# State products of the heads as 64-row tiles per head, on queries without zeros, even heads in one bank and odd heads in the other

## The chip, the cores and the metric

The kernel runs on one core of one Trainium2 chip. The metric is device time in microseconds of one execution; the time before is a median of three runs.

## The reference

One layer of a hybrid decoder over x (4096 tokens of 1024 values), cut here to what the change touches. The projection `h @ w_in` of the normalised input gives gated linear attention (GLA, 4 heads, 64 key and 128 value dimensions), a multi-scale pooling branch and a cross-attention into 256 memory tokens. The three are gated, concatenated, projected by `w_out`, added to x and normalised.

```python
# per head; chunks of 64 tokens; b = cumsum of the log decays in a chunk
q_d = q * exp(b)
k_d = k * exp(-b)
scores = tril(q_d @ k_d.T)                  # 64 x 64 in a chunk
o_intra = scores @ v
S_next = exp(b_last)[..., None] * S + k_end.T @ v   # S: 64 x 128
o_inter = q_d @ S                           # with the state before the chunk
o = o_intra + o_inter                       # then head RMSNorm, times silu(gate)
```

## The kernel before

The tokens go in 16 blocks of 256 (`TB`), each of 4 chunks of 64 (`NC`) and 2 halves of 128 tokens (`NT`). Blocks 0 to 3 are written out one by one and multiply whole weight matrices (`whole`, L683). Blocks 4 to 14 are one body in a loop on every engine, which multiplies by seven partial products a matrix (`phase` and `product`, L704); block 15 is written out with the tail behind it. The order on each engine is that of the code; engines wait for one another by semaphores.

The four heads are held as two pairs (`NPAIR`): of pair p, head 2p lies on partitions 0 to 63 and head 2p+1 on 64 to 127. Keys (`kd`), queries (`qb`) and the states `S[:, c, p, :]` (one for each chunk, 128 value columns) lie so. `qb` has a place for each head of a pair: `qb[:, p, h, :]` holds the decayed query of head h on its own 64 partitions and zeros on the other 64, which GpSimd writes once at the start (L2089). A product over all 128 partitions with `qb[:, p, h]` thus gives the one head alone.

In a block, TensorE (function `step`) works in this order behind the input products: values (`split`, L665), four transposes of `ke` (L866), the scores within chunks (L876, tiles of 64x64), scores against the memory (`mem_scores`, L892), a quarter of the output projection of the block before (`out_proj`, also L665), again L892, the chunk states (`states`, L903, tiles of 64x64), two more quarters, and then the stage that the change is about, `head_out`. For a pair p it multiplies the values by the masked scores `sT` (L912, o_intra, 4 products of f32) and the states by `qb` (L918, o_inter, 4 products of f32, 2 x 64 moving columns each), all added up in one bank: pair 0 in bank 5, pair 1 in bank 4. Behind it come the products of the memory attention (L971), the last quarter (L665) and the sums for the head norm (`head_ms`, L926).

ScalarE squares each of the two banks into `osq[p]` when the semaphore `pe_o` says so (L1425), and VectorE multiplies them by norm and gate into `mixed` (`head`, L1898 and L1900). VectorE makes `qb` (L1732), `ke` (L1735) and `kd` (L1737), and goes on with the states by `state` (L1889, semaphore `s_ok`). GpSimd waits for `pe_o` before it carries the last state over to the next block (L2138, L2139).

An f32 product of TensorE shows in the trace as two records of its line, each with its own weight load; so 4 products stand as x8.

Of the kernel before, what the change touches and what calls it, by code (L numbers as in the profile page):

```python
# [8 lines left out]
ALU = mybir.AluOpType  # L9
ACT = mybir.ActivationFunctionType  # L10
AX = mybir.AxisListType
F32 = mybir.dt.float32
# [4 lines left out]
P = 128  # L17
D = 1024
KT = D // P
TB = 256  # L20
NT = TB // P
CHUNK = 64
NC = TB // CHUNK
HEADS = 4
# [3 lines left out]
NPAIR = HEADS // 2  # L28
# [24 lines left out]
O_X, O_XS, O_MIX, O_T, O_U, O_QB = 0, 8192, 24576, 32768, 41216, 43392  # L53
# [55 lines left out]
def hybrid_block(nc, xt, x, memt, w_qk, w_v, w_qm, w_g, w_p, w_ut, w_gk_up, vecs, pool_w, counts, w_mem, w_out,  # L109
# [3 lines left out]
    with ctx:  # L113
# [3 lines left out]
        def sem(name):  # L117
            return ctx.enter_context(nc.semaphore(name))
# [33 lines left out]
        def view(off, shape, dt):  # L152

            size = int(np.prod(shape)) * (2 if dt in (F16, BF16) else 4)
            ap = arena[:, off // 4:(off + size) // 4]
            if dt != F32:
                ap = ap.bitcast(dt)
            if len(shape) == 2:
                ap = ap.rearrange("p (a b) -> p a b", b=shape[1])
            if len(shape) == 3:  # L160
                ap = ap.rearrange("p (a b c) -> p a b c", b=shape[1], c=shape[2])
            if len(shape) == 4:
                ap = ap.rearrange("p (a b c d) -> p a b c d", b=shape[1], c=shape[2], d=shape[3])
            return ap
# [8 lines left out]
        mixed = view(O_MIX, [KT, TB], F32)  # L173
# [4 lines left out]
        te = view(O_T + 6144, [2, TB], F32)  # L178
# [5 lines left out]
        pr = [view(O_T + 2048 * b, [2, NMEM], F32) for b in range(2)]  # L184
        phl = [view(O_T + 4096 + 2048 * b, [2, 2, NMEM], F16) for b in range(2)]
        ub = view(O_U, [2, HALO + TB], F32)
        qb = view(O_QB, [NPAIR, 2, TB], F32)
        kd = view(O_KD, [NPAIR, TB], F32)
        ke = view(O_KE, [NPAIR, TB], F32)
        osq = [view(o, [2, TB], F32) for o in (O_KD, O_KE)]  # L190
        v = view(O_V, [NT, 512], F32)
        gate = view(O_GATE, [KT, TB], F32)
# [4 lines left out]
        sT = view(O_ST, [NT, 2 * NPAIR, P], F32)  # L197
        S = view(O_S, [NC + 1, NPAIR, P], F32)
# [87 lines left out]
        bank = [ctx.enter_context(nc.psum_tensor(f"bank{i}", [P, 512], F32)) for i in range(8)]  # L286
# [10 lines left out]
        def col(n):  # L297
# [26 lines left out]
        built, ident_ok, zeroed, kept, mem_sq, mem_sum, mem_ms, mem_rs, mem_n = (  # L324
            sem(n) for n in ("built", "ident_ok", "zeroed", "kept", "mem_sq", "mem_sum", "mem_ms", "mem_rs",
                             "mem_n"))
# [13 lines left out]
        pe_o, pe_msq, pe_pv = (sem(n) for n in ("pe_o", "pe_msq", "pe_pv"))  # L340
# [6 lines left out]
        z_ok, gk_ok, b_ok, bl_ok, q_ok, dec_ok, kd_ok, ke_ok, pooled, y_add, y_ok = (  # L347
            sem(n) for n in ("z_ok", "gk_ok", "b_ok", "bl_ok", "q_ok", "dec_ok", "kd_ok", "ke_ok", "pooled",
                             "y_add", "y_ok"))
        sT_ok, max_ok, nmax_ok, rs_ok, s_ok, xn_ok, og_ok, mix_g, mix_m, mix_p, mmax_ok, m_lo = (  # L350
            sem(n) for n in ("sT_ok", "max_ok", "nmax_ok", "rs_ok", "s_ok", "xn_ok", "og_ok",
                             "mix_g", "mix_m", "mix_p", "mmax_ok", "m_lo"))
# [20 lines left out]
        def is_whole(i):  # L373
            return isinstance(i, int) and i < WHOLE
# [13 lines left out]
        def query(i):  # L388
            return qwhole if is_whole(i) else qtmp
# [212 lines left out]
        def _(pe):  # L602
# [146 lines left out]
            def step(i, first, second, last):  # L749
# [8 lines left out]
                for r in range(2):  # L758
                    for half in range(2):
                        for g in range(4):  # L760
                            k = 2 * g + half
                            b = 2 * (k // 4)
                            rhs = xs[:, 0, r, b:b + 2, (k % 4) * P:(k % 4 + 1) * P]
                            mm = nc.tensor.matmul(bank[3][32 * g:32 * g + 32, 0:TB], wlr[:, k, :], rhs,  # L764
                                                  start=r == 0 and half == 0, stop=r == 1 and half == 1)
# [13 lines left out]
                for j in range(2):  # L779
                    mm = nc.tensor.matmul(bank[5][:, j * TB:(j + 1) * TB], up4[:, j * P:(j + 1) * P],  # L780
                                          lrs[:, :], start=True, stop=True)
# [81 lines left out]
                for t in range(NT):  # L863
                    for p in range(NPAIR):
                        n = t * NPAIR + p
                        mm = nc.tensor.transpose(bank[4][:, n * P:(n + 1) * P], ke[:, p, t * P:(t + 1) * P],  # L866
                                                 ident[:, :])
                mm.then_inc(pe_ket, 1)
                for t in range(NT):
                    for p in range(NPAIR):  # L870
                        n = t * NPAIR + p
                        for odd in range(2):
                            for h in range(2):
                                r = slice(64 * h, 64 * h + 64)
                                c = slice((2 * t + odd) * CHUNK, (2 * t + odd + 1) * CHUNK)
                                mm = nc.tensor.matmul(bank[6 + h][64 * odd:64 * odd + 64, n * CHUNK:(n + 1) * CHUNK],  # L876
                                                      kd[r, p, c], qb[r, p, h, c], start=True, stop=True,
                                                      skip_group_check=True)
                mm.then_inc(pe_sc, 1)

# [24 lines left out]
                                                      start=True, stop=True, skip_group_check=True)  # L905
                    return mm

                def head_out(p, b):

                    for t in range(NT):  # L910
                        for h in range(2):
                            nc.tensor.matmul(bank[b][:, h * TB + t * P:h * TB + (t + 1) * P],  # L912
                                             v[:, t, (2 * p + h) * DV:(2 * p + h + 1) * DV],
                                             sT[:, t, 2 * p + h, :], start=t == 0 and h == 0, stop=False,
                                             skip_group_check=True)
                    o3 = bank[b][:, :].rearrange("p (h t) -> p h t", h=2)
                    for c in range(NC):
                        mm = nc.tensor.matmul(o3[:, :, c * CHUNK:(c + 1) * CHUNK], S[:, c, p, :],  # L918
                                              qb[:, p, :, c * CHUNK:(c + 1) * CHUNK], start=False,
                                              stop=c == NC - 1, skip_group_check=True)  # L920
                    mm.then_inc(pe_o, 1)

                def head_ms(p):

# [31 lines left out]
                pe.wait_ge(sT_ok, 2 * i + 1)  # L956
                pe.wait_ge(sT_ok, 2 * i + 2)
                pe.wait_ge(s_ok, 4 * i + 3)
                head_out(0, 5)
                pe.wait_ge(s_ok, 4 * i + 4)  # L960
                head_out(1, 4)
                for turned in d_turn:
                    pe.wait_ge(turned, 32 * (i + 1))
                pe.wait_ge(p_exp, 4 * i + 3)
# [1 line left out]
                for p in range(NPAIR):  # L966
                    for m in range(MT):
                        for n, (a, b) in enumerate(((0, 0), (0, 1), (1, 0))):
                            for h in range(2):
                                c = (2 * p + h) * 64  # L970
                                mm = nc.tensor.matmul(bank[2][64 * h:64 * h + 64, p * TB:(p + 1) * TB],  # L971
                                                      vm[:, a, m, c:c + 64], pt[:, p, (b * 2 + h) * MT + m, :],
                                                      start=m == 0 and n == 0, stop=m == MT - 1 and n == 2)
# [506 lines left out]
        def _(dve):  # L1480
# [170 lines left out]
            def step(i, first, second, last):  # L1651
# [71 lines left out]
                    add_2(i, QK)  # L1723
                dve.wait_ge(ad[QK], 4 * (i + 1))
                dve.wait_ge(ex_ok, 3 * i + 1)
                if first:
                    dve.wait_ge(zeroed, 1)
                else:
                    dve.wait_ge(pe_o, 2 * i)
                for h in range(2):  # L1730
                    r = slice(64 * h, 64 * h + 64)
                    nc.vector.tensor_tensor(qb[r, :, h, :], query(i)[r, :, :], te[r, :, :], ALU.mult).then_inc(q_ok, 1)  # L1732
                nc.vector.tensor_copy(dec[:, :, :], te[:, :, CHUNK - 1:TB:CHUNK]).then_inc(dec_ok, 1)
                dve.wait_ge(ex_ok, 3 * i + 3)
                nc.vector.tensor_tensor(ke, kd, tm, ALU.mult).then_inc(ke_ok, 1)  # L1735
# [2 lines left out]
                if first:  # L1738
# [27 lines left out]
                    for h in range(2):  # L1766
                        r = slice(64 * h, 64 * h + 64)
# [78 lines left out]
                def masked(h):  # L1846

                    if first:
                        dve.wait_ge(built, 3)
                        dve.wait_ge(zeroed, 2)  # L1850
                    dve.wait_ge(pe_sc, i + 1)
                    nc.vector.memset(idle[:, h:h + 1], 0.0)
                    for odd in range(2):
                        r = slice(CHUNK * odd, CHUNK * odd + CHUNK)
                        a = nc.vector.copy_predicated(s_head[r, :, h, r], mask[odd],
                                                      bank[6 + h][r, 0:256].rearrange("p (a b) -> p a b", b=CHUNK))
                    a.then_inc(sT_ok, 1)
# [36 lines left out]
                def head(p, b):  # L1894

                    dve.wait_ge(gate_out, 2 * i + 1)
                    dve.wait_ge(o_st, 4 * i + 2 * p + 2)
                    nc.vector.tensor_tensor(osq[p], osq[p], gate[:, 2 * p:2 * p + 2, :], ALU.mult).then_inc(og_ok, 1)  # L1898
                    dve.wait_ge(og_ok, 2 * i + p + 1)
                    nc.vector.tensor_tensor(mixed[:, 2 * p:2 * p + 2, :], bank[b][:, :].rearrange("p (a t) -> p a t", a=2),  # L1900
                                            osq[p], ALU.mult).then_inc(mix_g, 1)

                def rows(n):
# [105 lines left out]
        def _(pool):  # L2009
# [76 lines left out]
                    ins.then_inc(cb_ok, 1)  # L2086

            nc.gpsimd.memset(ub[:, :, 0:HALO], 0.0).then_inc(halo_ok, 1)
            nc.gpsimd.memset(qb, 0.0).then_inc(zeroed, 1)  # L2089
            x_begin(0)  # L2090
            pool.wait_ge(lo_c, LATER[QK] + 4)
            pool.wait_ge(lo_lr, 1)
# [105 lines left out]
```

## Time and profile before

| what | value |
|---|---|
| median of 3 runs | 1385.68 us (1384.72 to 1386.3) |
| the profiled execution | 1386.14 us, of which the span is 1384.3 us |
| TensorE busy (PE) | 1357.1 us, 98% |
| weight loads (PEld) | 1015.7 us, 73% |
| VectorE, ScalarE, GpSimd busy | 58%, 54%, 27% |
| L912 and L918, busy | 33.8 us each, in 256 records each |

PE are the products, PEld the weight loads that TensorE does beside them, DVE is VectorE, ACT ScalarE, POOL GpSimd. Busy times are of records that overlap within an engine, so the time that a stage takes is read from the starts of its rows and of the row behind it, not from the lengths.

### The profile page before, as it was taken

The numbers are of one execution on the slowest core, as the hardware profiler recorded it, in microseconds if no ns is written. First come the engines' busy times: TensorE is split into PE (matmuls) and PEld (weight loads), VectorE is DVE, ScalarE is ACT, GpSimd is POOL, SyncE is SP. The second block draws the span as 40 slices with busy tenths as digits, with TensorE's granted clock in tenths as the row PEclk, the third lists the DMA queues.
The fourth block names the chain that finished last, engine by engine and source line by source line (L and its number), as shares of the span: only waits on it lengthen the run. The fifth ranks groups of instructions, "written<-read, shape, count | busy, mean of one in ns | idle before, by whom it ended". The sixth has DMA issues, their size and how long they took to land.

```text
span 1384.3 us, 35236 instructions
## 1 busy us (share of the span) xinstructions
PE 1357.1 (98%) x14716; PEld 1015.7 (73%) x14716; DVE 796.9 (58%) x1524; ACT 753.6 (54%) x1380; POOL 370.7 (27%) x313
## 2 busy tenths in 40 slices
PE   6999999999999999999999999999999999999997
PEld 5788668576695968769586785958768596876953
DVE  5876567575554654554555555565555455555454
ACT  7886545655545464454646545464554556455352
POOL 2120164135323142332223223222332313233100
PEclk9999999999999999999999999999999999999999
DMA  9476556663673737456383654638366373745731
GB/s 387 174 209 214 213 183 215 199 242 137 203 255 94 275 107 260 183 180 240 95 294 123 242 201 147 251 97 290 132 209 249 116 265 97 262 177 183 254 83 46
DMA packets 143623, 269.31 MB, mean 195 GB/s; under 512 B 75137, under 2 KB 88705, under 8 KB 140417
## 3 DMA queue, kind: packets, MB, share of 16 engines
q1 hardware_dynamic: 142768, 266.20, 56.3%
q8 instruction: 116, 1.90, 0.5%
q10 hardware_dynamic: 720, 1.06, 0.2%
q14 instruction: 19, 0.15, 0.0%
HBM read 220.03 MB, written 30.41 MB: 181 GB/s over the span
## 4 chain that ended last, share of the span: by engine, by line
PE 94%; DVE 3%; ACT 2%; DMA 1%; issue 0%; SPq 0%; DVEq 0%; ACTq 0%
PE bank L665 34%; PE bank L704 33%; PE bank L683 10%; PE bank L892 2%; PE bank L918 2%; PE bank L912 2%; PE bank L926 2%; PE bank L971 2%; PE bank L994 2%; PE bank L903 1%; PE bank L780 1%; PE bank L876 1%; DMA out_parts<-fg 1%; PE bank L607 1%; DVE arena L1578 1%; PE bank L764 1%
## 5 line engine op out<-in xcount | busy, mean ns | idle before, releaser
L665 PE MATMUL bank<-ring,arena 128*128 128x512 f16 x1440 | 318.4, 379 | 0.0
L665 PEld LDWEIGHTS bank<-ring,arena 128*128 128x128 f16 x1440 | 138.5, 98 | 165.6 <-issue 5.9
L704 PE MATMUL bank<-arena,ring 128*128 128x128 f16 x4032 | 237.1, 219 | 0.0
L704 PE MATMUL bank<-arena,wres 128*128 128x128 f16 x4032 | 237.0, 219 | 0.0
L704 PEld LDWEIGHTS bank<-arena,ring 128*128 128x128 f16 x4032 | 228.4, 98 | 5.2 <-DVE arena L1556 1.9
L704 PEld LDWEIGHTS bank<-arena,wres 128*128 128x128 f16 x4032 | 227.7, 98 | 2.5 <-issue 2.5
L665 PE MATMUL bank<-wv,arena 128*128 128x512 f16 x768 | 170.2, 382 | 1.1 <-DVE wv L1542 1.1
L2029 POOL TENSOR_TENSOR arena<-arena 128x1024 f32<-128x1024 f32 (+2 forms) x42 | 64.8, 1543 | 355.1 <-ACT arena L1042 352.9
L665 PEld LDWEIGHTS bank<-wv,arena 128*128 128x128 f16 x768 | 75.5, 98 | 91.3 <-issue 2.3
L2037 POOL TENSOR_TENSOR arena<-arena 128x1024 f16<-128x1024 f32 x32 | 67.5, 2131 | 200.1 <-ACT arena L1060 200.1
L1637 DVE SCALAR_TENSOR_TENSOR arena<-bank,sca,arena 128x512 f32<-128x512 f32 x60 | 45.0, 749 | 111.1 <-DMA arena<-in_x 92.2
L1562 DVE SCALAR_TENSOR_TENSOR arena<-bank,sca,arena 128x256 f32<-128x256 f32 x48 | 23.2, 484 | 113.9 <-ACT arena L1148 113.9
L683 PE MATMUL bank<-arena,wres 128*128 128x256 f16 x768 | 86.1, 273 | 0.4 <-DVE wres L1520 0.4
L683 PE MATMUL bank<-arena,ring 128*128 128x256 f16 x768 | 85.3, 273 | 0.0
L1861 DVE TENSOR_REDUCE mx<-bank 128x2 f32<-128x512 f32 x64 | 41.1, 684 | 72.1 <-PE bank L892 72.0
L683 PEld LDWEIGHTS bank<-arena,wres 128*128 128x128 f16 x768 | 74.8, 98 | 10.3 <-DVE wres L1520 0.6
L683 PEld LDWEIGHTS bank<-arena,ring 128*128 128x128 f16 x768 | 75.1, 98 | 8.8 <-issue 0.2
L1873 DVE SCALAR_TENSOR_TENSOR arena<-arena,rsum 128x256 f16<-128x256 f32 x128 | 54.9, 482 | 43.3 <-ACT arena L1381 43.3
L1148 ACT ACTIVATE arena<-bank,sca 128x256 f32<-128x256 f32 x48 | 22.7, 473 | 97.3 <-PE bank L704 97.3
L2044 POOL TENSOR_TENSOR arena<-arena 128x512 f16<-128x512 f32 x48 | 58.1, 1219 | 55.0 <-ACT arena L1069 55.0
L1371 ACT ACTIVATE arena<-bank,nm,sca 128x256 f32<-128x256 f32 x128 | 71.0, 559 | 3.0
L1381 ACT ACTIVATE arena<-arena,rsum 128x256 f16<-128x256 f32 x128 | 55.9, 500 | 15.4 <-DVE rsum L1867 15.4
(247 smaller groups left out, 2004.6 us busy)
## 6 DMA issues: line engine op xcount, KB each, us to landing
ring<-out_parts SPq DMA_DIRECT2D x120, 512.0 KB, 5.5
ring<-gate_parts SPq DMA_DIRECT2D x92, 512.0 KB, 5.8
ring<-side_parts SPq DMA_DIRECT2D x92, 512.0 KB, 6.5
arena<-in_xt SPq DMA_DIRECT2D x16, 1024.0 KB, 6.8
arena<-in_x SPq DMA_DIRECT2D x32, 512.0 KB, 4.4
out<-arena SPq DMA_DIRECT2D x31, 512.0 KB, 2.9
arena<-in_w_out SPq DMA_DIRECT2D x16, 512.0 KB, 5.4
out_parts<-arena SPq DMA_DIRECT2D x6, 512.0 KB, 6.7
```

The source lines that it names most:

```text
L665: mm = nc.tensor.matmul(ap, lhs, rhs, start=k == 0 and n == 0, stop=(k, n) == last)
L683: mm = nc.tensor.matmul(ap, whole_parts[g][c][:, p, k % 4, j * P:(j + 1) * P], xs[:, 0, r, q:q + 2, (k % 4) * P:(k % 4 + 1) * P], start=k ...
L704: mm = nc.tensor.matmul(ap, w[:, p, k, j * P:(j + 1) * P], x_part(r, b)[:, k, :], start=fresh and j == 0 and k == 0 and n == 0, stop=k == ...
L892: mm = nc.tensor.matmul(bank[b][:, h * NMEM:(h + 1) * NMEM], qst[:, p, h, t * P:(t + 1) * P], kst[:, p, h, r, :], start=r == 0, stop=r == 1)
L1371: a = nc.scalar.activation(pr[n % 2][:, h, :], bank[2 + n % 2][:, h * 256:(h + 1) * 256], ACT.Exp, bias=nm[:, 2 * n + h:2 * n + h + 1], sc ...
L1381: a = nc.scalar.activation(phl[n % 2][:, 0, h, :], pr[n % 2][:, h, :], ACT.Copy, scale=rsum[:, 2 * n + h:2 * n + h + 1])
L1637: nc.vector.scalar_tensor_tensor(yb[:, c], bank[h][:, :], sc_out, yb[:, c], ALU.mult, ALU.add).then_inc(y_add, 1)
L1861: nc.vector.tensor_reduce(mx[:, 2 * n:2 * n + 2], bank[2 + n % 2][:, :].rearrange("p (h m) -> p h m", h=2), AX.X, ALU.max).then_inc(max_ok, 1)
L1873: a = nc.vector.scalar_tensor_tensor(phl[n % 2][:, 1, h, :], pr[n % 2][:, h, :], rsum[:, 2 * n + h:2 * n + h + 1], phl[n % 2][:, 0, h, :], ...
L2029: nc.gpsimd.tensor_tensor(sq[:, 0:half, :], sq[:, 0:half, :], sq[:, half:2 * half, :], ALU.add).then_inc(sq_add, 1)
L2037: nc.gpsimd.tensor_tensor(ap[1], xb[:, 4 * k:4 * k + 4, :].rearrange("p k (b t) -> p k b t", b=2), ap[0], ALU.subtract).then_inc(x_lo, 1)
L2044: nc.gpsimd.tensor_tensor(x_part(1, b), sg[(m - 3) % 2], x_part(0, b), ALU.subtract).then_inc(x_lo, 1)
```

## The change

The queries lose their zeros: `qb` has one place a pair, made by one instruction over all 128 partitions, and GpSimd's fill goes. The product with the states is made for each head by itself over its 64 partitions, 16 products of 64 rows by 128 weight columns with 64 moving columns, in place of 8 of 128 rows with 2 x 64. The even heads (partitions 0 to 63) go to bank 5, the odd ones to bank 4; the products by the scores (L912) are put in the same banks, and stand ahead of all the state products. The readers of the two banks take heads 0 and 2, and 1 and 3.

```diff
-        qb = view(O_QB, [NPAIR, 2, TB], F32)
+        qb = view(O_QB, [NPAIR, TB], F32)
...
-                                                      kd[r, p, c], qb[r, p, h, c], start=True, stop=True,
+                                                      kd[r, p, c], qb[r, p, c], start=True, stop=True,
...
-                def head_out(p, b):
+                def head_rows(h):
 
                     for t in range(NT):
-                        for h in range(2):
-                            nc.tensor.matmul(bank[b][:, h * TB + t * P:h * TB + (t + 1) * P],
+                        for p in range(NPAIR):
+                            nc.tensor.matmul(bank[5 - h][:, p * TB + t * P:p * TB + (t + 1) * P],
                                              v[:, t, (2 * p + h) * DV:(2 * p + h + 1) * DV],
-                                             sT[:, t, 2 * p + h, :], start=t == 0 and h == 0, stop=False,
+                                             sT[:, t, 2 * p + h, :], start=t == 0 and p == 0, stop=False,
                                              skip_group_check=True)
-                    o3 = bank[b][:, :].rearrange("p (h t) -> p h t", h=2)
+
+                def head_states():
+
                     for c in range(NC):
-                        mm = nc.tensor.matmul(o3[:, :, c * CHUNK:(c + 1) * CHUNK], S[:, c, p, :],
-                                              qb[:, p, :, c * CHUNK:(c + 1) * CHUNK], start=False,
-                                              stop=c == NC - 1, skip_group_check=True)
-                    mm.then_inc(pe_o, 1)
+                        for p in range(NPAIR):
+                            for h in range(2):
+                                r = slice(64 * h, 64 * h + 64)
+                                n = p * TB + c * CHUNK
+                                mm = nc.tensor.matmul(bank[5 - h][:, n:n + CHUNK], S[r, c, p, :],
+                                                      qb[r, p, c * CHUNK:(c + 1) * CHUNK], start=False,
+                                                      stop=c == NC - 1 and p == NPAIR - 1, skip_group_check=True)
+                                if c == NC - 1 and p == NPAIR - 1:
+                                    mm.then_inc(pe_o, 1)
...
-                head_out(0, 5)
+                head_rows(0)
                 pe.wait_ge(s_ok, 4 * i + 4)
-                head_out(1, 4)
+                head_rows(1)
+                head_states()
...
-                if first:
-                    dve.wait_ge(zeroed, 1)
-                else:
+                if not first:
                     dve.wait_ge(pe_o, 2 * i)
-                for h in range(2):
-                    r = slice(64 * h, 64 * h + 64)
-                    nc.vector.tensor_tensor(qb[r, :, h, :], query(i)[r, :, :], te[r, :, :], ALU.mult).then_inc(q_ok, 1)
+                nc.vector.tensor_tensor(qb, query(i), te, ALU.mult).then_inc(q_ok, 2)
...
-                    nc.vector.tensor_tensor(osq[p], osq[p], gate[:, 2 * p:2 * p + 2, :], ALU.mult).then_inc(og_ok, 1)
+                    nc.vector.tensor_tensor(osq[p], osq[p], gate[:, p:HEADS:2, :], ALU.mult).then_inc(og_ok, 1)
...
-            nc.gpsimd.memset(qb, 0.0).then_inc(zeroed, 1)
```

On TensorE, in the loop body, the stage stands so before, with the semaphores that an instruction waits for; behind it are the products of the memory attention (L971):

```order
324 L912 MATMUL bank<-arena 128x128 [waits s_ok,sT_ok]
325 L912 MATMUL bank<-arena 128x128 x3
326 L918 MATMUL bank<-arena 128x2x64 x4
327 L912 MATMUL bank<-arena 128x128 [waits s_ok]
328 L912 MATMUL bank<-arena 128x128 x3
329 L918 MATMUL bank<-arena 128x2x64 x4
330 L971 MATMUL bank<-arena,vm 64x256 [waits p_exp,d_turn1,d_turn0]
```

and so with the change, where the state products are L924 and the memory attention is L979:

```order
320 L912 MATMUL bank<-arena 128x128 [waits s_ok,sT_ok]
321 L912 MATMUL bank<-arena 128x128 x3
322 L912 MATMUL bank<-arena 128x128 [waits s_ok]
323 L912 MATMUL bank<-arena 128x128 x3
324 L924 MATMUL bank<-arena 128x64 x16
325 L979 MATMUL bank<-arena,vm 64x256 [waits p_exp,d_turn1,d_turn0]
```

The eight products L912 now stand together, the second wait for `s_ok` comes four products sooner, and 16 small products follow in place of two times 4.

On VectorE, in the loop body, the making of queries and keys before:

```order
367 L1732 TENSOR_TENSOR arena<-arena 64x2x256 [waits pe_o,ex_ok]
368 L1732 TENSOR_TENSOR arena<-arena 64x2x256
369 L1733 COPY dec<-arena 128x8
370 L1735 TENSOR_TENSOR arena<-arena 128x512 [waits ex_ok]
371 L1736 REGISTER_ALU
372 L1737 TENSOR_TENSOR arena<-arena 128x512 [waits ex_ok]
```

and with the change, where L1736 is the query product:

```order
363 L1736 TENSOR_TENSOR arena<-arena 128x512 [waits pe_o,ex_ok]
364 L1737 COPY dec<-arena 128x8
365 L1739 TENSOR_TENSOR arena<-arena 128x512 [waits ex_ok]
366 L1740 REGISTER_ALU
367 L1741 TENSOR_TENSOR arena<-arena 128x512 [waits ex_ok]
```

One instruction over 128 partitions stands where two over 64 stood; what is ahead of and behind it is the same.

## Rows read from the trace of the kernel before

**Rows 1.** The page: span, busy times, granted clock, chain; pieces of the chain (start, us)

```profile
span 1384.3 us, 35236 instructions
PE 1357.1 (98%) x14716; PEld 1015.7 (73%) x14716; DVE 796.9 (58%) x1524; ACT 753.6 (54%) x1380; POOL 370.7 (27%) x313
PEclk9999999999999999999999999999999999999999
PE 94%; DVE 3%; ACT 2%; DMA 1%; issue 0%; SPq 0%; DVEq 0%; ACTq 0%
656.95 10.36 PE bank L665 x48
739.00 10.36 PE bank L665 x48
```

**Rows 2.** Waits of TensorE over the whole span: us in total, times, longest

```profile
PE bank L653 <- DVE sca L1591: 6.5, 1, 6.5
...
PE bank L926 <- ACT arena L1425: 1.0, 1, 1.0
```

**Rows 3.** Timeline of TensorE's products in a loop block: start, us, instructions

```profile
749.73 0.69 PE L876 MATMUL bank<-arena 64*64 64x64 f32 x32
750.36 1.05 PE L892 MATMUL bank<-kst,arena 128*128 128x256 f16 x8
751.24 5.34 PE L665 MATMUL bank<-ring,arena 128*128 128x512 f16 x24
756.42 1.04 PE L892 MATMUL bank<-kst,arena 128*128 128x256 f16 x8
757.39 1.10 PE L903 MATMUL bank<-arena 64*64 64x128 f32 x32
758.42 10.53 PE L665 MATMUL bank<-ring,arena 128*128 128x512 f16 x48
768.79 1.05 PE L912 MATMUL bank<-arena 128*128 128x128 f32 x8
769.69 1.06 PE L918 MATMUL bank<-arena 128*128 128x128 f32 x8
770.58 1.06 PE L912 MATMUL bank<-arena 128*128 128x128 f32 x8
771.47 1.06 PE L918 MATMUL bank<-arena 128*128 128x128 f32 x8
772.46 1.50 PE L971 MATMUL bank<-arena,vm 128*64 128x256 f16 x24
773.89 5.35 PE L665 MATMUL bank<-ring,arena 128*128 128x512 f16 x24
779.08 1.45 PE L926 MATMUL bank<-arena,ones 128*128 128x512 f32 x3
```

**Rows 4.** Weight loads by line and shape: busy us, mean ns, idle before

```profile
L918 PEld LDWEIGHTS bank<-arena 128*128 128x128 f32 x256 | 31.2, 192 | 0.0
...
L971 PEld LDWEIGHTS bank<-arena,vm 128*64 128x64 f16 x384 | 19.7, 110 | 1.9
L903 PEld LDWEIGHTS bank<-arena 64*64 64x64 f32 x512 | 13.8, 132 | 3.4 <-issue 3.4
...
L876 PEld LDWEIGHTS bank<-arena 64*64 64x64 f32 x512 | 8.9, 134 | 2.7 <-issue 2.7
...
L764 PEld LDWEIGHTS bank<-arena,wlr 128*32 128x32 f16 x256 | 5.4, 95 | 11.6 <-issue 11.4
```

**Rows 5.** Timeline of block 0: f32 products with one moving column

```profile
80.59 0.30 PEld L612 LDWEIGHTS bank<-sca,ones 128*128 128x128 f32 x2
80.70 0.28 PE L612 MATMUL bank<-sca,ones 128*128 128x1 f32 x2
80.81 0.30 PEld L613 LDWEIGHTS bank<-sca,ones 128*128 128x128 f32 x2
...
81.07 0.27 PE L683 MATMUL bank<-arena,ring 128*128 128x256 f16 x1
```

**Rows 6.** Timelines of VectorE, ScalarE and GpSimd beside the stage

```profile
719.72 1.40 DVE L1732 TENSOR_TENSOR arena<-arena 64x512 f32<-64x512 f32 x2 [0.20 <-DVE arena L1570]
721.24 0.68 DVE L1735 TENSOR_TENSOR arena<-arena 128x512 f32<-128x512 f32 x1
765.84 1.31 DVE L1889 SCALAR_TENSOR_TENSOR arena<-arena,dec,bank 128x128 f32<-128x128 f32 x4
772.57 0.60 ACT L1425 ACTIVATE arena<-bank 128x512 f32<-128x512 f32 x1 [1.19 <-PE bank L918]
2.56 0.94 POOL L2089 MEMSET arena<- 128x1024 f32 x1
17.80 2.13 POOL L2037 TENSOR_TENSOR arena<-arena 128x1024 f16<-128x1024 f32 x1 [14.30 <-ACT arena L1060]
```

More of the change, by code:

```diff
@@ L1849, in masked @@
                         dve.wait_ge(built, 3)
-                        dve.wait_ge(zeroed, 2)
+                        dve.wait_ge(zeroed, 1)
                     dve.wait_ge(pe_sc, i + 1)
@@ L1897, in head @@
                     dve.wait_ge(o_st, 4 * i + 2 * p + 2)
-                    nc.vector.tensor_tensor(osq[p], osq[p], gate[:, 2 * p:2 * p + 2, :], ALU.mult).then_inc(og_ok, 1)
+                    nc.vector.tensor_tensor(osq[p], osq[p], gate[:, p:HEADS:2, :], ALU.mult).then_inc(og_ok, 1)
                     dve.wait_ge(og_ok, 2 * i + p + 1)
-                    nc.vector.tensor_tensor(mixed[:, 2 * p:2 * p + 2, :], bank[b][:, :].rearrange("p (a t) -> p a t", a=2),
+                    nc.vector.tensor_tensor(mixed[:, p:HEADS:2, :], bank[b][:, :].rearrange("p (a t) -> p a t", a=2),
                                             osq[p], ALU.mult).then_inc(mix_g, 1)
```

## The prediction

> **What bounds the kernel now.** I read the page's busy shares first: TensorE is busy 98% of a span of 1384.3 us, VectorE 58%, and the granted clock stays in its top tenth, the 2.4 GHz level, in all 40 slices [rows 1]. The chain that ended last is 94% TensorE, and in it the same piece of work comes back after 82.05 us (656.95 and 739.00), the period of a loop block [rows 1]. Then the waits of TensorE: the longest is 6.5 us, once, at the start; the only one near the changed code is 1.0 us, once, at L926 [rows 2]. The reader is to see that after the start nothing holds TensorE up: it goes from block to block without a gap. A nanosecond added to or taken from TensorE's queue is a nanosecond of the kernel, 16 times over, and work taken from VectorE or GpSimd is worth nothing unless TensorE waits for it.
>
> Last I read TensorE's queue in one loop block [rows 3]. The changed stage runs from the first L912 at 768.79 to the first L971 at 772.46: 3.67 us, 59 us in 16 blocks. Each x8 is 4 instructions of two passes, since an f32 product shows two records, and takes 0.89 to 0.90 us (768.79, 769.69, 770.58, 771.47), so 0.112 us a pass. The last x8 takes 0.99: 0.10 more, at the point where the shape goes from `128*128` to `128*64`.
>
> **What the change costs.** The 8 products L912 keep their shapes; they only stand together now: 16 passes, 1.79 us, as before. The 8 products of the states (each 128 rows, 2 x 64 moving columns, half of them against zeros) become 16 of 64 rows and 64 moving columns. The multiplying shrinks to a quarter if the two row halves run at the same time. The question is whether multiplying is what takes the time.
>
> Two facts come from the trace. First, separate tiles do run side by side. L876 has 16 products of 64x64x64 in 32 records, and 0.63 us passes to L892 (749.73 to 750.36) [rows 3]. Less 0.10 for the change of shape behind it and 0.05 for a first load that nothing hides, that is 0.48 for eight groups of four, 0.06 a group. L903 does eight such groups with 128 moving columns in 1.03 us: less 0.15, 0.11 a group. Four tiles' loads and products lie over one another, among them tiles in both row halves.
>
> Second, a weight load has a length of its own. Load records last 95 ns for 32 columns of f16, 110 ns for 64, 132 to 134 ns for 64 columns of f32, and 192 ns for 128 columns of f32 [rows 4]. So 64 more f32 columns cost about 59 ns, 0.92 ns a column, twice the f16 rate of 15/32 = 0.47. The f32 load of 64 columns has only 64 rows, and it falls where the rates put it (192 less 60): fewer rows made it no shorter. The load is hidden under a product of 128 columns because both take 0.11 us. What happens when the product is short can be read in block 0, where L612 and L613 multiply one single moving column by 128 columns of f32 weights. The two loads of L612 start at 80.59 and those of L613 at 80.81 [rows 5]: 0.22 us for two passes, 0.11 a pass, for a product with nothing to stream. The products follow at that pace (the next line's first is at 81.07, 0.37 after the first of L612, with four passes between whose first load was hidden). With 128 columns of f32 weights a pass costs 0.11 us however few columns move.
>
> The new products keep the 128 weight columns (the value dimension) and halve only rows and moving columns. So I price a pair, one tile in each row half, at one load, 0.112 us, not at the 0.058 of its product. 16 products x 2 passes / 2 side by side = 16 pair passes = 1.79 us. That is what the 8 old products cost in 16 passes. The halves that run together only pay for there being twice as many loads.
>
> The Trainium skill, TensorE: Matmul & The Clock Gate, section LDWEIGHTS, says the same against this change: a load's time goes by its columns and not by the contraction rows. By that page's figure, 128 columns divided by 1.2, a load is 107 ns, an estimate by which the stage comes out within 0.1 us of mine. The trace agrees, with its 0.11.
>
> What is new is the change of tile shape between L912 and L924. Before, the stage stayed at `128*128` throughout. The price has two parts. The drain: L892 before L903 takes 0.97 (756.42 to 757.39), but 0.88 (750.36 to 751.24) before a line of the same shape [rows 3], so 0.09. The first load, which nothing hides after a drain: 0.11 for 128 f32 columns by the spacing in [rows 5] (L903 shows the same with 64 columns: eight groups of 0.11 leave 0.15 of its 1.03, which is 0.10 of exit and 0.05 of first load). Against that the last product before L971 is short, 0.06 in place of 0.11: -0.05. The exit to `128*64`, 0.10, is paid before and after.
>
> Stage after: 1.79 + 0.09 + 0.11 + 1.79 - 0.05 + 0.10 = 3.83 us, against 3.67: +0.16 a block, +2.5 us in 16.
>
> **What lies beside it.** VectorE's query product goes from two of 64 rows (1.40 us the pair) to one of 128 rows, which I price at 0.68, the next 128x512 f32 row [rows 6]. That is 0.7 us less a block on an engine that TensorE doesn't wait for there: 0. GpSimd's 1024-column fill at the start goes; after it GpSimd is idle for 14.30 us [rows 6]: 0. The wait for the last state update now stands 0.89 us earlier in TensorE's queue; the update (L1889) starts at 765.84 and lasts 1.31 us, so it is over 1.6 us before even the first L912 [rows 6]: 0. It is cover that would have to shrink by 2.5 us before it cost anything.
>
> The signal for the first bank now comes with that for the second, some 1.9 us later. ScalarE's two squares (0.60 us each) then start at about 772.6 and end by 773.8; TensorE asks for them at 779.08 [rows 3, 6]. In the last block the sums stand right behind the 24 products L971 (1.43 us, 772.46 to 773.89 here), and two squares take 1.2: just covered, and worth 0.1 at worst. In block 0 the wait of 1.0 [rows 2] hangs on a second square that ScalarE comes to late in any case, so I leave it as it is.
>
> The sum is made against the profiled execution: 1386.14 us with a span of 1384.3. That is 0.46 above the median of the three runs, 1385.68. The change adds the same to either: 1386.14 + 2.5 = 1388.6, and for the median **1388.2 us**.
>
> **Bounds of the likeliest case.** Low: drain and first load hidden by TensorE's look-ahead, as no change of shape in this trace shows, gives -0.05 a block, 1384.9. High: a pair pass of 0.117 (0.005 each for a second issue) adds 0.08, so +0.24 a block, 1389.5.
>
> **Rivals.**
> Products bound, not loads. If a load of 64 rows took half of the 0.11, or if two tiles' weights were ahead by enough, a pair would cost 0.058, as a group of L876 does. The stage would be 1.79 + 0.09 + 0.05 + 0.93 + 0.10 = 2.96, -0.71 a block, -11.4 us: 1374.3. For it: L876 loads 128 weight columns into each row half in 0.06 us. Against: it does so through two column tiles of 64, each of which has a load of its own, and the one-column passes of [rows 5] show the full width at 0.11. The Trainium skill, TensorEngine Tiling (Array Packing), section Theoretical Speedup, promises up to twofold for a contraction of 64; halving the stage's second part is this rival. 9 in 100.
>
> The tiles don't overlap. If loads of 128 columns in the two halves follow one another, 32 passes of 0.112 give 3.58 in place of 1.79: with the 0.16 it is +1.95 a block, +31 us: 1416.9. It decides from the point at which two loads share less than nine tenths of their time (a tenth of 1.79 x 16 is 2.9 us, over the bound of what can be measured). For it: no `64*128` tile stands in the trace. Against: L876 and L903 load both halves at once. 5 in 100.
>
> A new wait: squares or a semaphore late in each block, so that TensorE stops at L926. The cover is some 5.3 us (773.8 to 779.08) and would have to vanish; 4 in 100 with all else, either sign.
>
> **How the numbers follow.** The likeliest case has 82 in 100. A measurement of this kernel tells about 0.2%, 2.8 us, from no change: slower begins at 1388.5, just above my figure. I give 52 of the 82 to within and 30 to slower, as 0.02 us a block moves it across. With the rivals: faster 0.10, same 0.52, slower 0.38. The range is 1384.5 to 1390.5, the likeliest case's bounds with a little for the median's own spread (1384.72 to 1386.3); both large rivals lie outside it, 14 in 100 together.
>
> **What would show it.** In the profile after: L912 as one x16 of 1.79 us; a gap of 0.2 between its last start and the first L924; 32 records of L924 in pairs a few ns apart, pairs 0.11 apart, load records of about 190 ns; first L912 to first PV product 3.8 us. Pairs 0.06 apart prove the first rival, single records 0.11 apart the second. I am wrong as well if the block's period (82.05 us) moves by anything but the stage.

## The result, and the profile after

The changed kernel takes 1388.21 us in the median of 14 runs, against 1385.38 us in as many of the kernel before: a ratio of 1.0018 (95% interval 1.001 to 1.0025), or 2.5 us with 1.4 to 3.5 as its interval; the medians themselves lie 2.8 apart. The profiled execution has a span of 1387.6 us, 3.3 more than before.

The page's lines after, to be read against [rows 1]: span, busy times, granted clock and the chain by engine.

```profile
span 1387.6 us, 35735 instructions
PE 1358.0 (98%) x14972; PEld 1017.1 (73%) x14972; DVE 783.2 (56%) x1508; ACT 753.0 (54%) x1380; POOL 368.4 (27%) x312
PEclk9999999999999999999999999999999999999999
PE 87%; DVE 5%; ACT 4%; issue 2%; DMA 1%; SPq 0%; ACTq 0%; DVEq 0%
```

VectorE has 13.7 us less to do, and it bought nothing. The chain is 87% TensorE where it was 94%: it now leaves TensorE in each loop block for ScalarE and VectorE, which the section on the reasons comes back to.

The stage in a loop block, TensorE's products (start, us), answers to the last rows of [rows 3]; and the load records of the new line answer to [rows 4].

```profile
771.04 1.95 PE L912 MATMUL bank<-arena 128*128 128x128 f32 x16
772.92 2.00 PE L924 MATMUL bank<-arena 64*128 64x64 f32 x32
774.85 1.50 PE L979 MATMUL bank<-arena,vm 128*64 128x256 f16 x24
...
L924 PEld LDWEIGHTS bank<-arena 64*128 64x128 f32 x512 | 29.8, 188 | 1.9
```

The reader is to see that L912 takes 1.88 us up to the next start, L924 1.93, together 3.81 in place of 3.67. The 32 records of L924 take as long as the 16 of L918 did and a little more, although, two tiles side by side, they have half as many columns to stream. Their loads last 188 ns, as long as those of 128 rows (192): half the rows made no load shorter.

The period of a loop block, from two pieces of the chain (start, us):

```profile
659.06 10.36 PE bank L665 x48
...
741.25 10.36 PE bank L665 x48
```

That is 82.19 us against 82.05. Sixteen times 0.14 to 0.15 is 2.3 of the 3.3 us between the two spans. The other 1.0 us lies in blocks 0 and 1, where TensorE's wait for VectorE at L607 is 6.6 us in all against 5.6 before. In the profiles of the experiments below the first L912 of block 1 comes anywhere between 183.7 and 188.2 us, in kernels whose work up to there differs by less than 1 us, so I take that part for scatter of single executions and not for the change.

### The profile page after: what moved, and what is told of

Its sections match the earlier page's. It is cut to its first block, busy times and chain, and to the rows that moved or that the text cites. A ratio compares the mean times of both kernels' runs of the same rounds, so it can differ in the third digit from the quotient of the medians.

```text
span 1387.6 us, 35735 instructions
## 1 busy us (share of the span) xinstructions
PE 1358.0 (98%) x14972; PEld 1017.1 (73%) x14972; DVE 783.2 (56%) x1508; ACT 753.0 (54%) x1380; POOL 368.4 (27%) x312
## 3 DMA queue, kind: packets, MB, share of 16 engines
q8 instruction: 118, 1.93, 0.6%
## 4 chain that ended last, share of the span: by engine, by line
PE 87%; DVE 5%; ACT 4%; issue 2%; DMA 1%; SPq 0%; ACTq 0%; DVEq 0%
PE bank L665 34%; PE bank L704 26%; PE bank L683 10%; PE bank L924 2%; PE bank L892 2%; PE bank L912 2%; DVE arena L1634 2%; PE bank L933 2%; ACT arena L1176 2%; PE bank L979 2%; PE bank L1002 2%; PE bank L903 1%; PE bank L780 1%; ACT arena L1150 1%; PE bank L876 1%
## 5 line engine op out<-in xcount | busy, mean ns | idle before, releaser
L665 PE MATMUL bank<-ring,arena 128*128 128x512 f16 x1440 | 318.4, 379 | 0.0
L665 PEld LDWEIGHTS bank<-ring,arena 128*128 128x128 f16 x1440 | 138.6, 98 | 165.5 <-issue 5.9
L665 PE MATMUL bank<-wv,arena 128*128 128x512 f16 x768 | 170.0, 381 | 1.1 <-DVE wv L1550 1.1
L665 PEld LDWEIGHTS bank<-wv,arena 128*128 128x128 f16 x768 | 75.4, 98 | 91.4 <-issue 2.2
```

The lines of the kernel that those rows point to most:

```text
L665: mm = nc.tensor.matmul(ap, lhs, rhs, start=k == 0 and n == 0, stop=(k, n) == last)
```

## The experiments

All are compared with the kernel before in the same sitting, with the number of runs given.

### VectorE's query product in two halves again

```diff
-                nc.vector.tensor_tensor(qb, query(i), te, ALU.mult).then_inc(q_ok, 2)
+                for h in range(2):
+                    r = slice(64 * h, 64 * h + 64)
+                    nc.vector.tensor_tensor(qb[r, :, :], query(i)[r, :, :], te[r, :, :], ALU.mult).then_inc(q_ok, 1)
```

> The changed kernel with one thing undone: VectorE makes the query product in two instructions of 64 rows again. Main theory (VectorE's saving is worth nothing, because a chain through ScalarE and VectorE ends at TensorE's second side product in each loop block whatever VectorE does earlier): the time of the changed kernel, 1388.2 us within 0.7; TensorE's stop ahead of the first side product (0.13 us, seen before) comes back and its stop ahead of the second shrinks from 0.30 to about 0.16, the block's period stays 82.19 us. Rival (the saving is real): about 0.13 us a block more, 1390 us or above.

Measured: 1388.35 us (11 runs), ratio to before 1.0018 (1.0009 to 1.0027), the same as with the whole change. VectorE's 0.7 us a block is worth nothing here. To see why, take TensorE's products of the input matrices in a loop block; each line has 72 passes and needs 4.02 us. First of the kernel before, then of the changed one, then of this experiment:

```profile
719.28 4.18 PE L704 MATMUL bank<-arena,wres 128*128 128x128 f16 x72
723.43 4.19 PE L704 MATMUL bank<-arena,ring 128*128 128x128 f16 x72
727.46 4.18 PE L704 MATMUL bank<-arena,wres 128*128 128x128 f16 x72
731.64 4.19 PE L704 MATMUL bank<-arena,ring 128*128 128x128 f16 x72
```

```profile
721.52 4.18 PE L704 MATMUL bank<-arena,wres 128*128 128x128 f16 x72
725.54 4.18 PE L704 MATMUL bank<-arena,ring 128*128 128x128 f16 x72
729.57 4.18 PE L704 MATMUL bank<-arena,wres 128*128 128x128 f16 x72
733.89 4.19 PE L704 MATMUL bank<-arena,ring 128*128 128x128 f16 x72
```

```profile
723.08 4.18 PE L704 MATMUL bank<-arena,wres 128*128 128x128 f16 x72
727.24 4.19 PE L704 MATMUL bank<-arena,ring 128*128 128x128 f16 x72
731.27 4.18 PE L704 MATMUL bank<-arena,wres 128*128 128x128 f16 x72
735.44 4.19 PE L704 MATMUL bank<-arena,ring 128*128 128x128 f16 x72
```

Start to start is 4.15, 4.03, 4.18 before; 4.02, 4.03, 4.32 after; 4.16, 4.03, 4.17 here. So there are two stops in a block that no row of waits of the products names: 0.13 us ahead of the second of these lines, 0.16 ahead of the fourth. With VectorE earlier the first goes and the second grows to 0.30. The waits of the weight loads do name the second, with an addition of VectorE as what ends it. Over the whole span, before and then after (us in total, times, longest):

```profile
PEld bank L704 <- DVE arena L1556: 1.9, 11, 0.2
...
PEld bank L704 <- DVE arena L1564: 3.4, 11, 0.3
```

Once in each of the 11 loop blocks, 0.17 us before and 0.31 after. From the second line's start to the fourth's, plus the first stop, it is 8.34 or 8.35 us in all three: something else than TensorE sets that length.

### The order alone

```diff
...
-                head_out(0, 5)
+                head_rows(0, 5)
                 pe.wait_ge(s_ok, 4 * i + 4)
-                head_out(1, 4)
+                head_rows(1, 4)
+                head_states(0, 5)
+                head_states(1, 4)
```

Made on the kernel before; `head_rows` holds its four score products of a pair, `head_states` its four state products on 128 rows with zeros.

> The kernel before with the order alone changed: all 8 score products first, then the 8 state products on 128 rows with zeros, same banks per pair. Main theory (order and later signal cost nothing, the loss is in the change of tile shape): 1385.4 us within 0.7, stage 3.67 us. Rival (the late signal for the first bank costs something, or the order does): up to 0.15 us a block more, 1387.8 us.

Measured: 1385.31 us (11 runs), ratio 0.9997 (0.9988 to 1.0006). TensorE's products in one block:

```profile
767.05 1.95 PE L912 MATMUL bank<-arena 128*128 128x128 f32 x16
768.84 1.95 PE L921 MATMUL bank<-arena 128*128 128x128 f32 x16
770.72 1.50 PE L976 MATMUL bank<-arena,vm 128*64 128x256 f16 x24
```

3.67 us as before. The order, the earlier wait and the late signal for the first bank are free; the 0.14 comes with the 64-row products. (The heads' new places in the banks and the fill that goes are not in this run.)

### Half of the moving columns

```diff
-                                mm = nc.tensor.matmul(bank[5 - h][:, n:n + CHUNK], S[r, c, p, :],
-                                                      qb[r, p, c * CHUNK:(c + 1) * CHUNK], start=False,
+                                mm = nc.tensor.matmul(bank[5 - h][:, n:n + CHUNK // 2], S[r, c, p, :],
+                                                      qb[r, p, c * CHUNK:c * CHUNK + CHUNK // 2], start=False,
```

This kernel leaves out the states' part for half of the tokens; it serves for the time alone.

> The changed kernel with 32 moving columns in place of 64 in each state product, so the states' part is left out for half of the tokens. Load theory: a pair of tiles stays at 0.112 us, since its length is the load of 128 weight columns; the stage stays 3.8 us (at most 0.03 less on the way out) and the time within 0.7 of 1388.2 us. Product theory (the moving columns set the length): pairs shrink by half, 0.9 us a block, 1374 us.

Measured: 1388.05 us (10 runs), ratio 1.0017 (1.0008 to 1.0027).

```profile
770.66 1.98 PE L924 MATMUL bank<-arena 64*128 64x32 f32 x32
772.57 1.50 PE L979 MATMUL bank<-arena,vm 128*64 128x256 f16 x24
```

1.91 us in place of 1.93, for half the streaming: what the products stream doesn't set their pace.

### Four tiles, by halves of the weight columns

```diff
                         for p in range(NPAIR):
-                            for h in range(2):
...
-                                mm = nc.tensor.matmul(bank[5 - h][:, n:n + CHUNK], S[r, c, p, :],
...
+                            for e in range(2):
+                                for h in range(2):
...
+                                    mm = nc.tensor.matmul(bank[5 - h][o, n:n + CHUNK], S[r, c, p, o],
...
```

`o` is `slice(64 * e, 64 * e + 64)`; the signal goes with e = 1.

> The changed kernel with each state product cut once more, into two of 64 weight columns, so that four 64x64 tiles share the array (32 products, 64 records). Load theory: a group of four tiles lasts as long as a load of 64 f32 columns, 0.058 us, so 16 groups take 0.94 us in place of 1.79 and the first load 0.05 in place of 0.11: stage 2.90 us in place of 3.81, 16 x 0.91 = 14.6 us less, 1373.6 us. Rival (something else holds a group at 0.11 us, the writing of two banks or the issue of records): 1388 us, or more with 64 records to issue.

Measured: 1375.27 us (5 runs), ratio 0.9923 (0.9909 to 0.9936), faster than the kernel before.

```profile
762.71 1.95 PE L912 MATMUL bank<-arena 128*128 128x128 f32 x16
764.58 1.16 PE L925 MATMUL bank<-arena 64*64 64x64 f32 x64
765.67 1.50 PE L980 MATMUL bank<-arena,vm 128*64 128x256 f16 x24
...
L925 PEld LDWEIGHTS bank<-arena 64*64 64x64 f32 x1024 | 16.4, 134 | 1.9
```

The same numbers are multiplied, in twice as many products, and L925 takes 1.09 us where L924 took 1.93. What each product covers has changed from 128 weight columns to 64, with four tiles in the array in place of two, and its load record from 188 ns to 134. Twice as many records in less time also rule out that the number of records sets the pace. Together with the run before it this is the cause shown from both sides: less streaming at the same width gives 0.02 us, half the width at the same streaming gives 0.84 us a block (16 x 0.84 = 13.4; the medians differ by 12.9). The stage is 2.96, not the 2.90 I expected: I had taken the savings from 3.81 without seeing that the last pair's short product was already in it. The sum of the prediction's first rival (also 2.96) had it right.

### One more way into the 64-row shape

```diff
...
-                head_rows(0)
+                head_rows(0, (0,))
                 pe.wait_ge(s_ok, 4 * i + 4)
-                head_rows(1)
-                head_states()
+                head_rows(1, (0,))
+                head_states((0, 1))
+                head_rows(0, (1,))
+                head_rows(1, (1,))
+                head_states((2, 3))
```

The arguments choose halves of 128 tokens and chunks.

> The changed kernel with the 64-row products done in two visits (score products of the first 128 tokens, their states, then the same for the second 128), so that one more way out of and into the 64-row shape is paid. Main theory: a way out costs 0.10 and a hidden first load of 0.11, a way in 0.09 and 0.11, less a short last product 0.05: 0.36 us a block more, 5.8 us, 1394.0 us. Rival (the change of shape is free and the loss lies elsewhere): 1388.2 us.

Measured: 1392.16 us (5 runs), ratio 1.0049 (1.0035 to 1.0063).

```profile
773.01 1.05 PE L912 MATMUL bank<-arena 128*128 128x128 f32 x8
773.99 1.11 PE L924 MATMUL bank<-arena 64*128 64x64 f32 x16
775.03 1.16 PE L912 MATMUL bank<-arena 128*128 128x128 f32 x8
776.12 1.11 PE L924 MATMUL bank<-arena 64*128 64x64 f32 x16
777.16 1.50 PE L982 MATMUL bank<-arena,vm 128*64 128x256 f16 x24
```

4.15 us for the stage, 0.34 more than 3.81, and 16 x 0.34 = 5.4; the medians differ by 4.0, with an interval that reaches from about 2 to 6. The first L912 takes 0.98 (0.89 and the drain of 0.09), the second 1.09: 0.11 more for a load that stands behind a drain with nothing to hide it.

### ScalarE's copies ahead of the squares

```diff
                     mixed_hi(i - 1)
+                    act.wait_ge(ad[GG], 4 * (i + 1))
+                    early_copies(i, PM)
                     if not last:
                         act.wait_ge(m_lo, i)
                         squares(i + 1)
-                    act.wait_ge(ad[GG], 4 * (i + 1))
-                    early_copies(i, PM)
```

> The changed kernel with ScalarE's two copies after the first side product placed ahead of the squares for the next block. Chain theory (in 11 loop blocks TensorE stops 0.30 us ahead of the second side product for a chain copies, cast, VectorE's remainder, squares, copy, addition): the stop goes, 11 x 0.30 = 3.3 us less than the changed kernel, 1384.9 us, period 81.89 us. Rival (the gap of 0.30 is how the shape or weights of that product start, not a wait): 1388.2 us.

Measured: 1385.43 us (11 runs), ratio to the kernel before 0.9999 (0.999 to 1.0008); against the changed kernel's 1388.21, from another sitting, that is 2.8 less, where 3.3 was expected.

```profile
717.58 4.18 PE L704 MATMUL bank<-arena,wres 128*128 128x128 f16 x72
721.60 4.18 PE L704 MATMUL bank<-arena,ring 128*128 128x128 f16 x72
725.62 4.18 PE L704 MATMUL bank<-arena,wres 128*128 128x128 f16 x72
729.63 4.18 PE L704 MATMUL bank<-arena,ring 128*128 128x128 f16 x72
```

4.02, 4.02, 4.01: both stops are gone, and the block's period is 81.88 us in place of 82.19. And with VectorE's product in two halves as well (the diff of the first experiment):

> The kernel of the run before it with VectorE's query product in two halves again. Chain theory: with the chain gone, VectorE's 0.7 us counts: TensorE's stop of 0.13 us ahead of the first side product comes back in 11 blocks, 1.4 us more than the run before, 1386.3 us. Rival (VectorE's saving is worth nothing even so): the same time as the run before.

Measured: 1386.83 us (11 runs), ratio 1.0012 (1.0003 to 1.0021), 1.4 above the run without the halves, as expected; the lines stand 4.16, 4.03, 4.02 apart. With the chain out of the way, VectorE's 0.7 us is worth 0.13 a block. In the changed kernel a second wait gives the same time back. On the kernel before, the copies alone:

> The kernel before with ScalarE's two copies placed early, and nothing else. Chain theory: TensorE's stop of 0.16 us ahead of the second side product goes in 11 loop blocks, that of 0.13 ahead of the first stays: 1.8 us less than the kernel before, 1383.9 us, period 81.89 us. Rival (the gaps are no waits): 1385.7 us.

Measured: 1384.65 us (11 runs), ratio 0.9996 (0.9987 to 1.0005). The block's period in the trace fell by 0.17 us, to 81.88, where 0.16 was expected; the total's interval holds both theories, so of the time this run tells nothing. The period is worth a second look: with the copies early it is 81.88 us before the change and 81.88 after it. There the change's 0.14 on TensorE and VectorE's saving cancel in the loop blocks.

### Together

> Column tiles and early copies together on the changed kernel. If the two are independent: 1388.2 - 14.6 - 3.3 = 1370.3 us. If the stage's gain moves the chain so that a new stop appears: up to 3.3 us more, 1373.6 us.

Four tiles and early copies: 1370.94 us (4 runs), ratio 0.9899 (0.9884 to 0.9914), within 0.7 us of the 1370.3 that the two expected gains add up to. The period is 81.04 us: 82.19 less 0.84 and 0.31. Then the score products in tiles too, half of them behind the memory attention:

```diff
+                                    h, b = (1 - odd, 4 + odd) if swap else (odd, 5 - odd)
...
+                                    mm = nc.tensor.matmul(bank[b][o, n:n + CHUNK], v[r, t, d:d + 64],
+                                                          sT[r, t, 2 * p + h, odd * CHUNK:(odd + 1) * CHUNK],
...
-                head_rows(0)
                 pe.wait_ge(s_ok, 4 * i + 4)
-                head_rows(1)
+                head_rows(False)
                 head_states()
...
+                pe.wait_ge(pe_hs, 2 * (i + 1))
+                head_rows(True)
```

`odd` is the chunk's half of 128 tokens, and `r` its 64 rows; `pe_hs` is a semaphore from the states, and GpSimd's carry waits for `pe_pv`.

> The column tiles and early copies of the run before, with the score products cut into 64x64x64 tiles too (the masked scores are zero between chunks, so only the blocks on the diagonal are multiplied): 32 products in place of 8, half of them ahead of the states, half behind the memory attention's products, since a row half must not write the other half's bank beside it. By the groups of 0.058 measured: from the first score product to the end of the second visit 0.09 + 0.05 + 0.47 + 0.94 + 0.10, memory attention 1.43, 0.05 + 0.47 + 0.10 = 3.70 us in place of 2.97 + 1.43 = 4.40: 16 x 0.70 = 11.2 us less than 1370.9, and about 1.2 more once in the last block where the squares now come late: 1360.9 us. Rival (the later signal for the squares or the second visit makes TensorE wait in each block): less than half of that gain, 1366 us or above.

Measured: 1367.12 us (4 runs), ratio 0.9872 (0.9857 to 0.9887), the fastest of all.

```profile
763.31 0.69 PE L917 MATMUL bank<-arena 64*64 64x64 f32 x32
763.83 1.11 PE L933 MATMUL bank<-arena 64*64 64x64 f32 x64
764.87 1.50 PE L987 MATMUL bank<-arena,vm 128*64 128x256 f16 x24
766.30 0.69 PE L917 MATMUL bank<-arena 64*64 64x64 f32 x32
766.93 5.35 PE L665 MATMUL bank<-ring,arena 128*128 128x512 f16 x24
```

In the loop blocks it went by the sum: 3.62 us from first L917 to L665, against 4.41 without it, and 0.09 more ahead of the first L917, where the shape now changes. The period is 80.35 us against 81.04. But only 3.8 us of the 10 expected came out. By its time alone this fits the rival (1366 us or above), but TensorE doesn't stop in each block, as the rival has it. One loop block lasted 81.57 us, with an idle of 1.0 ahead of a product L917 ("issue"); the rest was lost in the blocks written out. TensorE's waits name part of it (us in total, times, longest):

```profile
PE bank L683 <- DVE arena L1655: 3.3, 2, 1.6
PE bank L942 <- ACT arena L1443: 3.1, 3, 1.7
...
PE bank L987 <- issue: 1.1, 1, 1.1
PE bank L917 <- issue: 1.0, 1, 1.0
```

The squares (L1443) come late in block 0 (2.4 us of the 3.1, where the kernel without this order has 1.1) and in the last (0.7). The 3.3 us stand in the written-out blocks, on VectorE's additions of the output rows. None of the other eleven profiles has such a wait, but there is only one of this kernel, so whether it belongs to this order stays open.

## Why the prediction was right, point by point

**The bound.** The bound held and the size with it: 1388.2 forecast, 1388.21 measured. That they agree to 0.01 us is luck: medians of the kernel before lay between 1384.70 and 1385.79 us from one sitting to the next. But the sentence that nothing holds TensorE up after the start was wrong in detail, and it would have misled for another change. The list of waits counts idle time from the recorded end of the product ahead, and a record of 219 ns covers a gap of 160. The stops were visible in starts, 4.15 and 4.18 where 4.03 is the rule, and the second also in the waits of the weight loads, which [rows 2] does not hold. They belong to this chain, here as the critical chain of the changed kernel has it, with ScalarE's squares from its timeline as the last row:

```profile
725.81 0.47 ACT arena L1150
...
726.64 1.90 ACT arena L1176
...
728.57 2.36 DVE arena L1634
...
732.86 0.47 ACT arena L1150
...
733.35 0.50 DVE arena L1564
...
733.89 6.87 PE bank L704 x120
...
731.04 1.91 ACT L1050 ACTIVATE arena<-arena 128x2048 f32<-128x2048 f32 x1 [2.50 <-DVE arena L1634]
```

It starts when TensorE ends one product's first phase (725.5), goes through two copies, the cast, VectorE's remainder, the squares and a copy and an addition, and lets TensorE into the second side product at 733.89. Its 8.35 us are longer than the 8.04 that TensorE has to do meanwhile.

**VectorE's 0.7 us: 0.** Right in the sum, wrong in the reason. TensorE did wait for VectorE there, 0.13 us a block, and the saving removed that stop; the chain gave the same time back at the next one. The runs with the copies early show both halves. The zero thus came out by luck: nothing in the prediction knows of the chain, and without it the same saving would have taken back all that the change costs in a loop block, some 11 x 0.14 = 1.5 of the 2.5 us.

**The pair at one load, 0.112.** Confirmed: 32 records in 1.93 us, of which 0.16 at the start and 0.20 at the end leave 14 steps of 0.112. Halved streaming and halved width decide it between load and product. Two steps on the way to it were weaker than they looked. The multiplying shrinks to a half and not to a quarter when the row halves run together (16 pairs of 64 columns for 16 passes of 128), as the first rival's 0.93 for 1.79 has it. And that fewer rows made a load no shorter was read off a rate that came from that same load; the 188 ns of L924 show it directly.

**The drain and the first load.** L912 took 1.88 in place of 1.79: the drain of 0.09. For L924 the terms were 0.11 + 1.79 - 0.05 + 0.10 = 1.95, and 1.93 was measured. The stage was forecast at 3.83 and is 3.81; a block at +0.16, and it is +0.14.

**The hidden edits.** The earlier wait and the late signal: nothing, as the order alone shows. No run takes out GpSimd's fill or moves the heads between the banks by itself; the stage and the block's period leave nothing for them to explain in the loop.

**The rivals.** Products as the bound fell. Its stage of 2.96 us and its 1374.3 are what the four tiles then reached (2.96 and 1375.27), since it had priced a group at the time of L876, which also has four tiles. The rule of up to twofold in the Trainium skill, TensorEngine Tiling (Array Packing), section Theoretical Speedup, was not borne out for this shape: the measured factor of the states' part is 1.79 + 0.10 over 1.93, about 1. A factor near two came only with the weight columns halved as well, where 1.09 against 1.89 is 1.7. The rule of the Trainium skill, TensorE: Matmul & The Clock Gate, section LDWEIGHTS, that a load's time goes by its columns and not by its rows agrees with 188 ns for 64 rows and 192 for 128. Loads that follow one another fell too: pairs 0.112 apart are two loads in that time.

## What to carry to other kernels

Before cutting f32 products by rows, ask what their pace is: with 128 f32 weight columns a pass took 0.11 us however few rows or columns it used here, so only tiles that were narrower in the weights gained, and each change of tile shape cost 0.09 to 0.10 us for the drain and up to 0.11 for a load laid bare. Time stages by the starts of rows, and look at the waits of the weight loads as well as at those of the products: a stop shorter than a product's record is in no row of the products (here 0.13 to 0.30 us under 219 ns records), and of two such stops the loads' rows named one. Two stops in a row can make a saving ahead of them look worthless. A masked operand with zero blocks is a reason to look for small tiles on the diagonal.

## What the runs showed of the hardware

Two 64-row tiles with 128 f32 weight columns load side by side at no loss, 0.112 us for the pair, as long as one load of 128 rows. Four tiles of 64x64 took 1.09 us for 64 records with 0.15 for the way in and out, 0.059 a group. What I had not expected is that ScalarE and VectorE formed a chain of 8.35 us in each loop block, 0.3 us longer than TensorE's own work beside it, in a kernel where TensorE is busy 98% of the time.
